# The opening of a two-block decoder kernel: x loads, squares and key and query evacuations in another order

## The reference

```python
def rms_norm(x, w):
    xf = x.astype(jnp.float32)
    y = xf * lax.rsqrt(jnp.mean(xf * xf, axis=-1, keepdims=True) + EPS)
    return (y * w.astype(jnp.float32)).astype(x.dtype)
...
        n = rms_norm(h, attn_norm_w[l])
        proj = n @ w_in[l]
        aq, ak, av, rq, rk, rv, rg = jnp.split(proj, split_at, axis=-1)
        aq = rope(rms_norm(aq.reshape(B, S, ATTN_HEADS, HEAD_DIM), q_norm_w[l]), pos)
        ak = rope(rms_norm(ak.reshape(B, S, ATTN_KV_HEADS, HEAD_DIM), k_norm_w[l]), pos)
        av = av.reshape(B, S, ATTN_KV_HEADS, HEAD_DIM)
        y_attn = windowed_gqa_sink(aq, ak, av, attn_sink[l])
```

## Time and profile before

| | us |
|---|---|
| median of 3 runs | 2052.39 |
| range of the runs | 2051.28 to 2053.2 |
| profiled execution | 2050.78 |
| its span | 2049.0 |
| TensorE busy in the span | 2002.3 (98%) |
| VectorE, ScalarE, GpSimd busy | 828.0, 763.6, 742.0 |

### The profile page before, as it was taken

One profiled execution on the slowest core, in us unless ns is written; L12 is line 12 of the kernel. 1 busy time (PEld: TensorE's weight loads), 2 busy tenths in 40 slices (PEclk: granted clock), 3 DMA queues, 4 the chain that ended last, 5 costly groups with the idle time before them and its releaser, 6 DMA issues.

```text
span 2049.0 us, 27439 instructions
## 1 busy us (share of the span) xinstructions
PE 2002.3 (98%) x9460; PEld 1585.2 (77%) x9460; DVE 828.0 (40%) x1264; ACT 763.6 (37%) x1185; POOL 742.0 (36%) x295
## 2 busy tenths in 40 slices
PE   7999999999999999999989999999999999999999
PEld 5777778888888788878867776766788887888887
DVE  5677674332323534342383344444311264222200
ACT  5354343222223322322255555555422343322211
POOL 2221324444442344444423332222344433444443
PEclk9999999999999999999999999999999999999999
DMA  4111235553322555642212121111233322323322
GB/s 151 62 44 51 62 113 200 190 169 97 104 94 89 175 195 186 202 167 93 79 62 73 61 72 52 57 56 52 62 97 97 93 89 86 99 95 97 111 85 96
DMA packets 56643, 210.75 MB, mean 103 GB/s; under 512 B 6288, under 2 KB 7056, under 8 KB 56592
## 3 DMA queue, kind: packets, MB, share of 16 engines
q1 hardware_dynamic: 56592, 210.08, 31.6%
HBM read 207.96 MB, written 2.10 MB: 103 GB/s over the span
## 4 chain that ended last, share of the span: by engine, by line
PE 71%; issue 20%; POOL 4%; DVE 2%; ACT 2%; POOLq 0%; ACTq 0%; DVEq 0%
PE bank L414 62%; POOL wlo L369 4%; PE bank L448 2%; PE bank L759 1%; PE bank L774 1%; PE bank L785 1%; PE bank L694 1%; DVE xl L1389 1%; PE bank L794 1%; DVE sqn L1383 0%; ACT whi L863 0%; DVE wlo L1396 0%; ACT Dm L1213 0%; PE bank L470 0%; PE bank L766 0%
## 5 line engine op out<-in xcount | busy, mean ns | idle before, releaser
L369 POOL TENSOR_TENSOR wlo<-raw,whi 128x1024 fp32r<-128x1024 f32 (+1 forms) x290 | 738.9, 2548 | 1269.2 <-ACT whi L863 1269.2
L414 PE MATMUL bank<-xh,whi 128*128 128x512 f32 x1688 | 680.4, 403 | 19.5 <-DVE xl L1375 13.1
L414 PE MATMUL bank<-xh,wlo 128*128 128x512 f32 x1688 | 659.1, 390 | 0.0
L414 PE MATMUL bank<-xl,whi 128*128 128x512 f32 x1688 | 658.7, 390 | 0.0
L863 ACT ACTIVATE whi<-raw 128x1024 fp32r<-128x1024 f32 (+1 forms) x298 | 330.2, 1108 | 627.4 <-PE bank L414 614.0
L414 PEld LDWEIGHTS bank<-xh,whi 128*128 128x128 f32 x1688 | 317.7, 188 | 96.4 <-issue 21.1
L414 PEld LDWEIGHTS bank<-xl,whi 128*128 128x128 f32 x1688 | 318.2, 188 | 68.7 <-issue 6.7
L414 PEld LDWEIGHTS bank<-xh,wlo 128*128 128x128 f32 x1688 | 317.6, 188 | 68.0
L414 PE MATMUL bank<-acth,whi 128*128 128x512 f32 x528 | 209.0, 396 | 0.8 <-POOL wlo L369 0.8
L414 PE MATMUL bank<-acth,wlo 128*128 128x512 f32 x528 | 208.8, 395 | 0.0
L414 PE MATMUL bank<-actl,whi 128*128 128x512 f32 x528 | 208.8, 395 | 0.0
(11 more groups left out here) (304 smaller groups left out, 1958.9 us busy)
## 6 DMA issues: line engine op xcount, KB each, us to landing
raw<-w_dram SPq DMA_DIRECT2D x250, 512.0 KB, 3.6
adaw<-ada_dram SPq DMA_DIRECT2D x72, 512.0 KB, 4.4
raw<-wd_dram SPq DMA_DIRECT2D x48, 704.0 KB, 4.1
h<-x_dram SPq DMA_DIRECT2D x4, 512.0 KB, 7.2
out_dram<-h SPq DMA_DIRECT2D x8, 256.0 KB, 3.6
rel<-rel_dram SPq DMA_DIRECT2D x1, 513.0 KB, 7.8
crow<-c_dram SPq DMA_DIRECT2D x1, 512.0 KB, 3.5
gates_raw<-gates_dram SPq DMA_DIRECT2D x1, 384.0 KB, 8.3
```

Of the source, the lines that this page charges most:

```text
L369: nc.gpsimd.tensor_tensor(wlo[:, s, 0:width], raw[:, s, 0:width], whi[:, s, 0:width].bitcast(F32), ALU.subtract).then_inc(sem("w_lo"), 1)
L414: mm = nc.tensor.matmul(proj[b][:], w[:, s, W], v[:, k, :], start=first and j == 0 and a == 0, stop=last and j == len(chunks) - 1 and a == ...
```

## The change

Everything is in the first few dozen microseconds.

- SP loads all four parts of x right behind slab 0, then slab 1, then slab 2, which waits for the `wlo` of slab 0. The constants come behind that, and have three semaphores instead of one. The load of slab 3 is put ahead of that of the gates' weights.
- ScalarE makes all eight `xh` and the `whi` of slab 1 ahead of the squares. The squares go to eight places of their own (`first_squares`), one ahead of the evacuation of tile 0 and seven between its `split` and tile 1.
- VectorE moves the column preparations to the front, makes eight `xl`, then the `wlo` of slab 1 in place of POOL, and then six additions of squares.
- TensorE does 20 matmuls of `ones` by `ones`, 128 columns, into bank 7 first. Slab 0 runs unbroken. The norm's two matmuls stand in slab 2, behind two of its chunks, and go to bank 4.
- Keys and queries are evacuated by ScalarE straight from the bank, without `rstd`. Since the head norm divides out a factor per token, `rstd` isn't needed, but EPS changes its weight: VectorE adds the norm's sum, times a constant, to each tile's sum of squares (`rope_var`), and ScalarE takes the root of that with `eps2` as bias. The values are scaled by `rstd` as before (`local_values`).

```diff
             load_wide(None, 2, 0, 0)
-            load_x(0)
-            load_x(1)
+            for c in range(KC // 2):
+                load_x(c)
             load_wide(None, 2, 0, 1)
-            load_x(2)
-            load_x(3)
...
+            load_wide(None, 2, 2, 0)
+            load_const(blk, P, P, "turns_in")
...
+            load_wide(None, 2, 2, 1)
             sp.dma_start(gates_raw[:], gates_in).then_inc(sem("gates_in"), 16)
-            wide_loop(2, (SLAB["ff0"] - 2) // 2)
+            wide_loop(4, (SLAB["ff0"] - 4) // 2)
@@ TensorE
             def sums_and_turn(p):
 
-                pe.wait_ge(sem("rope_raw"), p + 1)
-                pe.wait_ge(sem("rope_out"), primed(p))
-                nc.tensor.matmul(bank[5][:], blk[:], rsq[:], start=True, stop=True).then_inc(sem("rope_ss"), 1)
+                pe.wait_ge(sem(f"evac{p % 2}"), primed(p // 2 + 1))
+                pe.wait_ge(sem("rope_out"), primed(max(p - 1, 0)))
+                nc.tensor.matmul(bank[5 + p % 2 * 2][:], blk[:], rsq[:], start=True, stop=True).then_inc(sem("rope_ss"), 1)
+                if p > 0:
+                    pe.wait_ge(sem("rope_part"), p * 2 - 1)
...
+            for _ in range(20):
+                nc.tensor.matmul(bank[7][:, 0:P], ones[:], ones[:], start=True, stop=True)
+
...
-                wide("att", 0, 2, p, part=(0, KC // 2))
+                if p == 2:
+                    wide("att", 0, 2, p, part=(0, 2))
+                    norm_sum(0, at=4)
+                    norm_sum_last(0, at=4)
+                    wide("att", 0, 2, p, part=(2, KC // 2))
+                else:
+                    wide("att", 0, 2, p, part=(0, KC // 2))
@@ ScalarE
                 z_high(0, c, attn_weight)
-                square_chunk(0, c, c % 2)
-                if c == 3:
-                    split(0, 2, 0, 1, WC)
-            act.wait_ge(sem("norm_sum"), primed(1))
-            inverse_root("norm", 0, bank[6][:], rstd[:], D)
+            split(0, 2, 0, 1, WC)
...
+            def first_norm():
+
+                act.wait_ge(sem("norm_sum"), primed(1))
+                nc.scalar.activation(ssum[:], bank[4][:], ACT.Copy).then_inc(sem("sumx"), 1)
+                inverse_root("norm", 0, bank[4][:], rstd[:], D)
 
             def rope_tile(p):
 
-                act.wait_ge(sem(f"evac{p % 2}"), primed(p // 2 + 1))
+                matmuls(p + 1)
                 act.wait_ge(sem("rope_out"), primed(max(p - 1, 0)))
-                nc.scalar.activation(rsq[:], pT[:, p % 2, :], ACT.Square)
-                nc.scalar.activation(rraw[:, p % 2, :], pT[:, p % 2, :], ACT.Identity,
-                                     scale=c1("q_norm" if p else "k_norm")).then_inc(sem("rope_raw"), 1)
+                nc.scalar.activation(rsq[:], proj[p % 2][:], ACT.Square)
+                nc.scalar.activation(rraw[:, p % 2, :], proj[p % 2][:], ACT.Identity,
+                                     scale=c1("q_norm" if p else "k_norm")).then_inc(sem(f"evac{p % 2}"), 1)
                 split(0, 2, 0, p + 2, WC)
 
             def rope_roots(p):
-                act.wait_ge(sem("rope_ss"), p + 1)
-                if p > 0:
-                    act.wait_ge(sem("rope_out"), primed(p))
-                inverse_root("rope", p, bank[5][:], rr[:], DH)
+                act.wait_ge(sem("rope_var"), p + 1)
+                nc.scalar.activation(rr[:], rr[:], ACT.Ln, scale=1.0 / DH, bias=eps2[:]).then_inc(sem("rope_ln"), 1)
...
+            first_square(0)
+            rope_tile(0)
+            for c in range(1, KC):
+                first_square(c)
+            rope_tile(1)
+            first_norm()
+            rope_roots(0)
@@ VectorE
+            for c in range(KC):
+                z_low(0, c, lambda m: c1("attn_norm", m))
+            dve.wait_ge(sem("w_lo"), primed(1))
+            dve.wait_ge(sem("w_hi"), 2)
+            V.tensor_tensor(wlo[:, 1, 0:WC], raw[:, 1, 0:WC], whi[:, 1, 0:WC].bitcast(F32), ALU.subtract).then_inc(sem("w_lo"), 1)
...
+            def rope_var(p):
+
+                dve.wait_ge(sem("rope_ss"), p + 1)
+                dve.wait_ge(sem("sumx"), 1)
+                V.scalar_tensor_tensor(rr[:], ssum[:], DH * EPS / D, bank[5 + p % 2 * 2][:], ALU.mult,
+                                       ALU.add).then_inc(sem("rope_var"), 1)
```

More of the change, by code:

```diff
@@ L116, in build @@
         epsc = sb("epsc", [P, 1])
+        eps2 = sb("eps2", [P, 1])
         shs = sb("shs", [P, 3, KC, 2], F32R)
@@ L381, in after_norm @@
                     pool.wait_ge(sem("w_lo"), primed(n + 4))
-            low_loop(0, SLAB["ff0"] + 2, WC)
+            pool.wait_ge(sem("w_hi"), 1)
+            nc.gpsimd.tensor_tensor(wlo[:, 0, 0:WC], raw[:, 0, 0:WC], whi[:, 0, 0:WC].bitcast(F32), ALU.subtract).then_inc(sem("w_lo"), 1)
+            pool.wait_ge(sem("w_lo"), primed(2))
+            low_loop(2, SLAB["ff0"], WC)
             after_norm(1)
@@ L421, in wide, with norm_sum, norm_sum_last @@
                      range(KC), ready=ready, part=part)
-            def norm_sum(r):
+            def norm_sum(r, at=6):
                 pe.wait_ge(sem("ssum"), primed((KC - 1) * (r + 1)))
-                nc.tensor.matmul(bank[6][:], ones[:], ssum[:], start=True, stop=False, skip_group_check=True)
-            def norm_sum_last(r):
+                nc.tensor.matmul(bank[at][:], ones[:], ssum[:], start=True, stop=False, skip_group_check=True)
+            def norm_sum_last(r, at=6):
                 pe.wait_ge(sem("sq"), KC * (r + 1))
-                nc.tensor.matmul(bank[6][:], ones[:], sqn[:, (KC - 1) % 2, :], start=False, stop=True,
+                nc.tensor.matmul(bank[at][:], ones[:], sqn[:, (KC - 1) % 2, :], start=False, stop=True,
                                  skip_group_check=True).then_inc(sem("norm_sum"), 1)
@@ L627, in mixing_step @@
                 ret_cross(t)
+            for _ in range(20):
+                nc.tensor.matmul(bank[7][:, 0:P], ones[:], ones[:], start=True, stop=True)
             for p in range(N_ATT):
                 if p == 0:
[L631 to L634, removed]
+                    wide("att", 0, 2, 0, ready=("z_lo", 0))
                     continue
-                wide("att", 0, 2, p, part=(0, KC // 2))
+                if p == 2:
[5 more added lines that the diff above has]
+                    wide("att", 0, 2, p, part=(0, KC // 2))
                 if p == 1:
-                    pe.wait_ge(sem("const_ready"), 1)
+                    pe.wait_ge(sem("turns_in"), 32)
                 sums_and_turn(p - 1)
                 if p == N_ATT - 1:
+                    pe.wait_ge(sem("const_ready"), 1)
                     win_scores(0, 0)
@@ L1024, in _ @@
             act.wait_ge(sem("q_scale"), 1)
-            for p in range(QT):
-                rope_tile(p)
+            first_square(0)
[5 more added lines that the diff above has]
+            rope_roots(0)
+            for p in range(1, QT):
+                if p > 1:
+                    rope_tile(p)
                 if p == QT - 1:
@@ L1029, in _ @@
                 rope_roots(p)
-                if p == 0:
+                if p == 1:
                     act.wait_ge(sem("rel_in"), 16)
@@ L1033, in _ @@
                     ret_key_decays()
[L1034 to L1035 removed]
+                ret_query_decays(p - 1)
             split(0, 2, 0, N_ATT + 1, WC)
@@ L1416, in _ @@
             V.memset(epsc[:], EPS)
+            V.memset(eps2[:], EPS * EPS)
             V.memset(ones[:], 1.0).then_inc(sem("ones"), 1)
-            clear_sum(0)
             dve.wait_ge(sem("cols_in"), 16)
-            for c in range(KC):
-                z_low(0, c, lambda m: c1("attn_norm", m))
-                if c < KC - 1:
-                    add_square(0, c, c % 2)
             V.tensor_scalar(lg[:], col[:, COL["decay_f"]:COL["decay_f"] + 2 * RH], -1.0, None, ALU.mult).then_inc(sem("lg"), 1)
@@ L1456, in rope_part @@
                     V.tensor_tensor(rt[:, 1, :], rraw[:, slot, :], cos[:], ALU.mult).then_inc(sem("rope_part"), 1)
+            def rope_var(p):
[3 more added lines that the diff above has]
+                                       ALU.add).then_inc(sem("rope_var"), 1)
             def normed_rope(p, dst):
+                if p == 0:
+                    dve.wait_ge(sem("angles_in"), 32)
                 for part in range(2):
                     rope_part(p, p % 2, 6, part)
+                rope_var(p)
                 dve.wait_ge(sem("rope_part"), p * 2 + 2)
@@ L1620, in _ @@
                 normed_rope(p, qall[:, p - 1, :] if p else kf[:])
-                att_scaled(p + 1)
+                if p == 0:
+                    const_casts()
+                if p == QT - 1:
+                    local_values()
                 if p == QT - 1:
```

47 lines of the change are left out of this document (29 added, 18 removed).

## The result

| | before | after |
|---|---|---|
| median, us | 2052.3 | 2038.39 |
| range | 2051.28 to 2053.2 (4 runs) | 2037.6 to 2038.98 (4 runs) |
| profiled execution, its span | 2050.78, 2049.0 | 2037.86, 2036.0 |
| matmuls with `acth`, `actl`, mean ns | 395 to 396 | 389 |

A forecast was written before the change was run, and what follows sets the result against it. TensorE's progress was taken as the bound, judged at the second probability tile: 6.0 us gained on slab 1, 6.4 given back, so +0.4, 2051.2 for the profiled execution and 2052.8 median; range 2049.3 to 2055.6.

The forecast's parts named there:

- the last stall of 1.9: TensorE waits 1.9 us for the second scaled probability tile, held by POOL's wlo, and passes at 66.43.
- A: The forecast itself: warm-up lost, slab 1 at 17.90, second probability tile 0.4 us later than before; chance 0.58.
- B: Rival: the warm-up holds the clock, slab 1 starts 1.55 us earlier; -1.15, median 2051.2; chance 0.2.
- (1): The norm's two matmuls move into slab 2: 1.86 us, plus a 0.4 stall at the norm's sum.
- (2): Keys' and queries' root waits for VectorE; TensorE waits 1.4 us for the evacuation of tile 2.
- (3): Steady-state closed loop through ScalarE and VectorE: 7.67 us against 7.31, losing 0.37 on each of two slabs.
- rival C: The loop does not close and evacuations keep up: stalls of 1.4 and 0.7 vanish, -1.7, 2050.7; chance 0.1.
- (4): Scores of block 0 at 56.1, values' transposes wait 0.9, second probability tile waits 1.9 and passes at 66.43.
- Rival D: Slower: the clock falls in the new stalls, 1.6 us per fall of eight matmuls; two give 2056.0; chance 0.06.

The follow-up runs named there:

- e1_before_pad: The kernel before with one unused 4-byte tile behind epsc, so acth and all tiles behind it start 32 bytes further on: 2037.31 us, ratio 0.9927 to before.
- e2_after_pad: The changed kernel with a second unused 4-byte tile behind eps2, putting acth and all behind it again 32 past a multiple of 64: 2054.43 us, ratio 1.0013 to before.
- o2_var_first: The changed kernel with the new sum of tiles 1 to 3 put ahead of VectorE's two products: 2033.14 us, ratio 0.9911 to before.
- o3_fill: The changed kernel with seven more matmuls of ones behind the first transposed probability tile, where TensorE waits 1.83 us: 2037.14 us.
- e3_x_off: The kernel before with unused 4-byte tiles ahead of xh and raw, so only xh and xl start 32 past a multiple of 64: 2077.89 us, ratio 1.0127.

## Why the prediction was wrong

**The step that failed** stands at the start: "The change touches the first 66 us only", and from it "All later work hangs on it at the same distances." I costed `eps2` as something that lies "beside waits". As an instruction it does. As an allocation it moved every tile behind it, and with them the pace of the 1584 matmuls of the down slabs and of those of the merge and output slabs. This one term is -15.8 by e1_before_pad (2037.31 against 2053.11) and -16.0 by e2_after_pad (2038.39 against 2054.43). I had no term for it in the sum, the range or the rivals, and the bound "For more than 4.1 of gain the last stall of 1.9 must go as well" rested on the same step. The rows would have shown a question: `acth` products at 396 ns and `xl` products at 390 on the page before, with one shape, no wait and one clock. I did not ask it. The last sentence of the prediction did name the sign by which to know: a difference over 4 us with the tile in place.

**The opening** came out near the forecast, and that is luck. I had +0.4 with the warm-up lost; the two pairs of kernels with equal tile places give +1.1 and +1.3. But the warm-up was not lost. TensorE was 0.45 ahead at the second probability tile, where A had it 0.4 behind and B 1.15 ahead, and in the profiled executions it is the falls of the clock that turn this into a loss. Misses of opposite sign nearly cancel. The terms:

- Slab 0: rival B came true, though not for its reason. It asked for a warm-up that ends near 10, 0.7 before slab 0. The warm-up ended at 7.91 (I had 7.4), TensorE was idle for 2.76, and the clock held all the same. Slab 1 started at 16.51 (B: 16.35).
- (1) The stall at the norm's sum: 0.20, I had 0.4.
- (2) The stall ahead of the third turn pair: 2.02 on `rraw` of ScalarE, I had 1.4. This and the later start of slab 1 make up the 0.7 by which B missed that tile. The norm's chain did start earlier, its copy at 27.59 (A 28.9, B 27.35). But the new sum of tile 0 stood on VectorE behind a product that ran beside POOL's `wlo` and took 2.75, not the 1.26 of the earlier trace rows:

```profile
26.25 2.37 POOL L379 TENSOR_TENSOR wlo<-raw,whi 128x1024 fp32r<-128x1024 f32 x1 [5.26 <-ACT whi L885]
26.43 2.75 DVE L1494 TENSOR_TENSOR rt<-rraw,cos 128x512 f32<-128x512 f32 x1
...
29.09 0.68 DVE L1500 SCALAR_TENSOR_TENSOR rr<-ssum,bank 128x512 f32<-128x512 f32 x1
...
29.80 0.72 ACT L974 ACTIVATE rr<-rr,eps 128x512 f32<-128x512 f32 x1 [0.37 <-DVE rr L1500]
```

  ScalarE waited 0.37 for that sum. Tile 2 began to be evacuated at 36.94, where B had 36.05.
- (3) The closed loop: turn pairs 45.77 - 38.15 = 7.62 apart, I had 7.67; rival C is out. The operation without a row, the new sum, took 0.68, the value I took, and stood behind a product held to 1.28 by POOL's `wlo` (the held value, 1.26). o2_var_first shows by undoing it that this order was the loop.
- (4) Scores at 55.31 (56.1, less B's 1.55: 54.6), values' transposes with 0.70 of wait (0.9), second probability tile at 65.55 with 1.83 (66.43 less 1.55: 64.9, with 1.9).
- Rival D came true once in the profiled execution: a fall behind the last stall, over twelve matmuls and not eight, 3.0 and not 1.6. e2_after_pad, which has the same stall and no fall, shows that it belongs to single executions.
- The lower end of the range, 2049.3, lies above the 2049.1 that it is said to run from. With 2038.39 measured this decides nothing.

This is VectorE, ScalarE and POOL in the profile after, around the third tile, for (3):

```profile
39.12 2.39 POOL L379 TENSOR_TENSOR wlo<-raw,whi 128x1024 fp32r<-128x1024 f32 x1 [10.49 <-ACT whi L885]
40.17 0.69 DVE L1492 TENSOR_TENSOR rt<-bank,sin 128x512 f32<-128x512 f32 x1 [3.77 <-PE bank L496]
40.78 1.28 DVE L1494 TENSOR_TENSOR rt<-rraw,cos 128x512 f32<-128x512 f32 x1
41.97 0.68 DVE L1500 SCALAR_TENSOR_TENSOR rr<-ssum,bank 128x512 f32<-128x512 f32 x1
42.69 0.73 ACT L974 ACTIVATE rr<-rr,eps 128x512 f32<-128x512 f32 x1 [3.65 <-DVE rr L1500]
```

My sentence on the Trainium skill ("TensorE: Matmul & The Clock Gate", section "Why this matters for your kernels", against long idle gaps) spoke against a warm-up that ends early. The runs show both sides: behind 6.79 us of warm-up the clock held over an idle time of 2.76, behind 6.39 (o3_fill) it fell in slab 0 after 3.58, and in the kernel before 2.41 had been enough.

## What to carry to other kernels

When a change adds, removes or resizes an SBUF tile, look where the tiles behind it come to lie before you say that only the edited stretch changes. If one group of matmuls is a few per cent slower than another of the same shape, with no wait and the same clock, compare the starts of the two operands. And test a surprising gain by adding an unused tile to the old kernel: one kernel separates the change from its side effect.

## What the runs showed of the hardware

- Reduced-fp32 matmuls with 512 columns at 2.4 GHz, each with a weight tile of its own, stood 0.227 us apart where the streamed tile and the weights start alike mod 64 (both at 0, or both at 32), and 0.233 where they start 32 bytes apart. Over the kernel this is 15.8 us for `acth` and its like, and 24.8 for `xh` and `xl` (e3_x_off, 2077.89 against 2053.11).
- One tile out of line costs two thirds of the full price or more: three products took 682 ns from start to start with all alike, 694 with `xl` alone out of line, 699 with `wlo` alone, 700 with `xh` and `xl`.
- The Trainium skill ("TensorE: Matmul & The Clock Gate", section "Wait — 56ns, not 53.3ns?") has 215.7 ns from start to start for 512 columns at the higher clock. The matmuls here, reduced fp32 and each with a weight load, do not come that close; both paces, 227 and 233 ns, lie above it, and the measurements decide here.
- The granted clock fell in some executions and not in others behind the same stall of 1.83 us: 0.52 over 67 to 74 us in the profile after, 1.00 in e2_after_pad. The fall cost 3.0 us. Differences of one to two us between two kernels of this size can be such falls, and only the traces tell them apart from the edit.
